# Order of the products in a 576-column matrix multiply, and matmuls that nobody reads in three pauses

## Chip, cores and metric

One core of one Trainium2 chip runs the whole program. The metric is the device time of one launch in microseconds, as a median of several launches: 2850.38 us for the kernel before (three runs, 2848.32 to 2852.73).

## What is computed

One inference step of a two-layer decoder, for a new sequence of 512 tokens and for 8 running sequences of 8 new tokens each. Both sets go through the same weights, so a block of activations has 576 token columns. The reference, cut to what matters:

```python
def _swiglu(h, w_in, w_out):
    gu = h @ w_in
    gate, up = gu[..., :D_FF], gu[..., D_FF:]
    return (jax.nn.silu(gate) * up) @ w_out

for i in range(DEPTH):                                   # DEPTH = 2, D_MODEL = 1024, D_FF = 2816
    x = x + 0.5 * _swiglu(_rms_norm(x, g1), ffn1_w_in[i], ffn1_w_out[i])
    h = _rms_norm(x, mix_norm[i])
    x = x + (gated_delta_net(h) if i < N_A else stick_breaking_attention(h))
    x = x + 0.5 * _swiglu(_rms_norm(x, g2), ffn2_w_in[i], ffn2_w_out[i])
    x = x + (p[i] @ ple_w_in[i]) * sigmoid(_rms_norm(x, gp) @ ple_w_gate[i])
```

After the first layer the shared keys and values are computed; the second layer attends to them and to 256 cached rows of each running sequence.

## The kernel before

**Layout.** Activations lie transposed: 128 of the 1024 features on the partitions, the 576 tokens along the free axis. A weight matrix is taken in blocks of 128 output features (`m` picks one of two output tiles in PSUM) and 128 input features (`k`, up to 8 per tile).

**Exactness.** Inputs are fp32. TensorE's quick type `fp32r` keeps fewer bits, so every operand is split into a high part and a remainder. ScalarE makes the weight's high part (`w_hi`, L462), VectorE the rest (`w_lo`, L477). The activations have the same two halves: `hx_hi` and `hx_lo` after a norm, `hid_hi` and `hid_lo` for a hidden block. A product is then the sum of three: high by high, high by low, low by high.

**The inner loop.** `multiply` (L503) runs over `k`. For each it waits for the activations of that `k` and issues the three products. 576 columns of fp32 don't fit one PSUM bank of 512, so each product is cut in two by `PARTS`: columns 0 to 320, which end one bank, and columns 320 to 576, which begin the next. That is six matmuls for each `k`, all summed into the same tile, and each comes with a weight load of its own. `multiply_pin` (L532) is the same for the embedding product, with 2 steps of `k`. While one tile is multiplied, the other is read out and its weights are split; `evac`, `w_lo_done` and `tile_done` count this.

**Where TensorE pauses.** The engines have queues in program order. In three places the queue of TensorE has nothing to do until others have finished:
- End of the gated DeltaNet stage (`gdn_pe`, L1783 to L1797): sums of squares of the outputs go to ScalarE, come back by token (L1787), go through a square root and a reciprocal, are turned (L1790, L1791), are split, and are spread over the partitions by `norm_spread` (L1474) and `sample_norm_spread` (L1480). VectorE scales the outputs head by head (L1454, L1456) and makes the remainder `hid_lo` (L1460). The first tile of the output projection is multiplied between these: after the product of head `k`, `norm_spread(k + 5)`.
- Start of attention (`attend_pe`, L2376 on): the scores of the first pair of heads and of the new tokens are done, and TensorE waits until ScalarE and GpSimd have turned them into `ls_hi` and `ls_lo` (L1969, L1919) before the suffix sums (`sums`, L2359 to L2362).
- End of attention (L2428 on): the last sequence's cached rows: `att_transposes` (L2297), `page_outputs` (L2310), `o_transposes` (L2319), then the output projection, which waits for `hid_lo` (L2153).

Of the kernel before, what the change touches and what calls it, by code (L numbers as in the profile page):

```python
# [21 lines left out]
P = 128  # L22
# [26 lines left out]
def program(nc, A, O):  # L49
# [33 lines left out]
    with ctx:  # L83
# [419 lines left out]
        def multiply(pe, s, u, m, between=None):  # L503

            k_all = (s.ka, s.kb)[m]
            hi, lo = s.rhs
            n = s.n["unit"]
            pe.wait_ge(w_lo_done, u * 2 + (2 * n + m + 1))
            if isinstance(u, int) and n + u == 0:
                pe.wait_ge(setup_ev, (3, EARLY_FILLS)[m])  # L510
            else:
                pe.wait_ge(evac[m], u + (n, s.n["eb"])[m])
            for k in range(k_all):
                if hi is hx_hi:
                    pe.wait_ge(hx_done, KD * (s.n["hx"] - 1) + k + 1)
                else:
                    pe.wait_ge(hid_done, s.n["hid"] - k_all + k + 1)
                if n + m == 1 and isinstance(u, int) and u == 0 and k == k_all // 2:
                    x_scale_rows(pe)
                if s.stats and n and isinstance(u, int) and u == m == 0 and k == k_all - 1:  # L520
                    pe_stats(pe, s, s.n["stat"])
                for a, (w, h) in enumerate(((w_hi, hi), (w_hi, lo), (w_lo, hi))):
                    for c0, c1 in PARTS:
                        last = nc.tensor.matmul(TILE[m][:, c0:c1], w[:, m, k], h[:, k, c0:c1],  # L524
                                                start=k == 0 and a == 0, stop=k == k_all - 1 and a == 2)
                if between:
                    between(k)
            last.then_inc(tile_done, 1)
            if s.kind == "ple":
                multiply_pin(pe, s, u, m)  # L530

        def multiply_pin(pe, s, u, m):  # L532

            j = KD * s.n["ple"] + m
            pe.wait_ge(pw_lo_done, u * 2 + (j + 1))
            pe.wait_ge(p_done, PK * (s.n["ple"] + 1))
            if not (isinstance(u, int) and 2 * u + j == 0):
                pe.wait_ge(ple_mul, u * 2 + j)
            hi, lo = PR
            for k in range(PK):  # L540
                for a, (w, h) in enumerate(((pw_hi, hi), (pw_hi, lo), (pw_lo, hi))):
                    for c0, c1 in PARTS:
                        last = nc.tensor.matmul(PIN[:, c0:c1], w[:, m, k], h[:, k, c0:c1],  # L543
                                                start=k == 0 and a == 0, stop=k == PK - 1 and a == 2)
            last.then_inc(pin_done, 1)

        def x_scale_rows(pe):

# [58 lines left out]
        def after(eng, *names):  # L607
            for name in names:
                eng.wait_ge(*order[name])
# [874 lines left out]
        def gdn_pe(pe, s):  # L1484
# [106 lines left out]
            def output_sums(heads_, n):  # L1591
                pe.wait_ge(g["osq"], 4 * n + 4)
                for half in range(2):
                    for x, h in enumerate(heads_):
                        last = mm(O_SUMS[32 * x:32 * x + 32, half], hot[:, 15 - h:47 - h], osq[h][:, half * HC:(half + 1) * HC],
                                  start=n == 0, stop=n == 1, skip_group_check=True)
                last.then_inc(g["osum"], 1)
# [31 lines left out]
            for hp in range(NG):  # L1629
# [115 lines left out]
                for i in range(PT):  # L1745
# [33 lines left out]
                    if (hp, i) == (3, 3):  # L1779
                        after(pe, "osum3_s")  # L1780
                        output_sums(FIRST_SUMS, 0)
                        sample_update(3, 7)
            output_sums(LAST_SUMS, 1)  # L1783
            after(pe, "osums")
            for i in range(NT):
                n = P if i < PT else TS
                last = mm(bank(2)[0:n, HA * i:HA * i + HA], o_sums[:, i * P:i * P + n], e32[:, 0:HA], start=True, stop=True)  # L1787
            done("o_by_token", last)
            after(pe, "orec0", "orec1")
            tr(bank(5)[0:32, 0:P], rs_c[:, 0:PT * HA], ident[:])  # L1790
            done("o_scale_rows", tr(bank(5)[0:HA, P:P + TS], rs_c[0:TS, PT * HA:], ident[0:TS, 0:TS]))  # L1791
            after(pe, "ilo0", "ilo1", "upd7_s")
            pe.wait_ge(g["ocp"], HA * PT)
            pe.wait_ge(g["su"], HA * PT)
# [435 lines left out]
        def attend_pe(pe, s):  # L2230
# [143 lines left out]
            far_scores(0)  # L2374
            new_scores()
            pe.wait_ge(at["made"], 5)  # L2376
            for n in range(NP):
                pe.wait_ge(at["lo"], 5 * n + 3)
                sums(n, 0, 2)
                sums(n, 1, 2).then_inc(at["r"], 1)  # L2380
                if n == 1:
                    k_transposes(0, 3)
                for a in range(2):
                    sums(n, a, 3)
                    sums(n, a, 1).then_inc(at["r"], 1)
                if n:
                    page_scores(n - 1)
                    k_transposes(n, 0)
                if n + 1 < NP:
                    near_scores(n + 1)  # L2390
                if n:
                    k_transposes(n, 1)
                for a in range(2):
                    pe.wait_ge(at["lo"], 5 * n + 4 + a)
                    sums(n, a, 0).then_inc(at["r"], 1)
                    if n == NP - 1:
                        k_transposes(n, 2 + a)
                if n == 0:
                    new_sums()
                elif n < NP - 1:  # L2400
                    k_transposes(n, 2)
                pe.wait_ge(hid_done, s.n["hid"] + n)
                pe.wait_ge(at["att"], 5 * n + 3)
                for b in (3, 2, 1):
                    weigh(n, b)
                if n == NP - 1:
                    page_scores(n)
                if n:
                    att_transposes(n - 1)
                if n + 1 < NP:  # L2410
                    far_scores(n + 1)
                if n:
                    page_outputs(n - 1)
                if 0 < n < NP - 1:
                    k_transposes(n, 3)
                pe.wait_ge(at["att"], 5 * n + 5)
                weigh(n, 0).then_inc(at["o_head"], 1)
                if n:
                    o_transposes(n - 1)
                else:  # L2420
                    new_outputs()
                    pe.wait_ge(at["new_out"], 2)
                    k_transposes(n, 0)
                    new_totals(range(0, NB // 2))
                    k_transposes(n, 1)
                    done("totn", new_totals(range(NB // 2, NB)))
                    k_transposes(n, 2)
            att_transposes(NP - 1)  # L2428
            page_outputs(NP - 1)
            o_transposes(NP - 1)  # L2430
            pe.wait_ge(at["o_lo_page"], 2 * NB)
            pe.wait_ge(hid_done, s.n["hid"] + KD)

# [746 lines left out]
```

## Time and profile before

| | |
|---|---|
| median of 3 runs | 2850.38 us |
| the profiled execution | 2854.08 us, span 2852.4 us |
| TensorE matmul, busy | 2768.1 us, 97% of the span, 20784 instructions |
| VectorE, ScalarE, GpSimd, busy | 1343.1, 952.1, 314.9 us |
| mean granted clock of TensorE | 0.984 of full speed |
| DMA | 79 GB/s in the mean, 16 engines about a quarter busy |

A profile of one execution is read here. Its lines name a source line, an engine, what is written and read, and how often. Matmuls are pipelined: a record reaches from the moment one enters the array until its result has drained, so records overlap. The distance between the starts of two is what one costs in a stream. "Granted clock" is the share of TensorE's full 2.4 GHz that the chip allowed at the time; it has two levels here, 1.00 and 0.50 (1.2 GHz). Where a row has brackets, they give the idle time of the engine before it and who ended it.

### The profile page before, as it was taken

The numbers are of one execution on the slowest core, as the hardware profiler recorded it, in microseconds if no ns is written. First come the engines' busy times: TensorE is split into PE (matmuls) and PEld (weight loads), VectorE is DVE, ScalarE is ACT, GpSimd is POOL, SyncE is SP. The second block draws the span as 40 slices with busy tenths as digits, with TensorE's granted clock in tenths as the row PEclk, the third lists the DMA queues.
The fourth block names the chain that finished last, engine by engine and source line by source line (L and its number), as shares of the span: only waits on it lengthen the run. The fifth ranks groups of instructions, "written<-read, shape, count | busy, mean of one in ns | idle before, by whom it ended". The sixth has DMA issues, their size and how long they took to land.

```text
span 2852.4 us, 49966 instructions
## 1 busy us (share of the span) xinstructions
PE 2768.1 (97%) x20784; PEld 2664.3 (93%) x20784; DVE 1343.1 (47%) x1694; ACT 952.1 (33%) x1365; POOL 314.9 (11%) x343
## 2 busy tenths in 40 slices
PE   8999999998999999999999999999989989999998
PEld 8999999997888899999999999999986689999998
DVE  4434347755545554343454434333546744333354
ACT  4212124453333332222342232222336832222243
POOL 2000002201234210000020000000132310000011
PEclk9999999999999899999999999999989999999999
DMA  5222322220011232322231432222212323222231
GB/s 136 74 81 81 89 70 92 77 79 20 18 32 32 91 87 76 88 82 80 74 102 61 135 88 82 81 88 74 89 45 82 131 84 89 83 80 88 74 100 53
DMA packets 308123, 225.71 MB, mean 79 GB/s; under 512 B 8270, under 2 KB 301567, under 8 KB 307967
## 3 DMA queue, kind: packets, MB, share of 16 engines
q1 hardware_dynamic: 307280, 224.26, 26.1%
q8 instruction: 67, 1.10, 0.2%
q14 instruction: 38, 0.31, 0.0%
q0 software_dynamic: 576, 0.00, 0.0%
q10 hardware_dynamic: 162, 0.04, 0.0%
HBM read 212.14 MB, written 12.13 MB: 79 GB/s over the span
## 4 chain that ended last, share of the span: by engine, by line
PE 62%; DVE 2%; ACT 1%; issue 1%; DMA 0%; POOL 0%; SPq 0%; DVEq 0%; POOLq 0%; ACTq 0%
PE ps L524 56%; PE ps L543 1%; PE ps L2325 1%; PE ps L2359 1%; DVE ls L2088 0%; PE ps L2264 0%; PE ps L2367 0%; PE ps L2310 0%; PE ps L1474 0%; PE ps L2361 0%; PE ps L2362 0%; DVE w_lo L477 0%; PE ps L2272 0%; PE ps L2332 0%; PE ps L2288 0%
## 5 line engine op out<-in xcount | busy, mean ns | idle before, releaser
L524 PE MATMUL ps<-hx_hi,w_hi 128*128 128x320 f32 (+1 forms) x3986 | 859.0, 297 | 6.2 <-DVE hx_lo L2453 5.5
L524 PE MATMUL ps<-hx_lo,w_hi 128*128 128x320 f32 (+1 forms) x3986 | 859.1, 296 | 0.0
L524 PE MATMUL ps<-hx_hi,w_lo 128*128 128x320 f32 (+1 forms) x3986 | 845.2, 293 | 0.0
L462 ACT ACTIVATE w_hi<-raw 128x1024 fp32r<-128x1024 f32 (+1 forms) x362 | 375.7, 1038 | 1235.7 <-PE ps L524 1234.9
L524 PEld LDWEIGHTS ps<-hx_lo,w_hi 128*128 128x128 f32 x3986 | 615.2, 190 | 0.0
L524 PEld LDWEIGHTS ps<-hx_hi,w_hi 128*128 128x128 f32 x3986 | 605.4, 188 | 9.9 <-issue 6.4
L524 PEld LDWEIGHTS ps<-hx_hi,w_lo 128*128 128x128 f32 x3986 | 609.7, 188 | 0.0
L477 DVE TENSOR_TENSOR w_lo<-raw,w_hi 128x1024 fp32r<-128x1024 f32 (+1 forms) x362 | 460.8, 1273 | 108.5 <-ACT w_hi L462 108.5
L524 PE MATMUL ps<-hid_hi,w_hi 128*128 128x320 f32 (+1 forms) x1664 | 359.9, 298 | 2.6 <-DVE hid_lo L2153 1.8
L524 PE MATMUL ps<-hid_lo,w_hi 128*128 128x320 f32 (+1 forms) x1664 | 358.6, 297 | 0.0
L524 PE MATMUL ps<-hid_hi,w_lo 128*128 128x320 f32 (+1 forms) x1664 | 357.2, 296 | 0.0
L2470 POOL TENSOR_TENSOR ssum<-ssum,sqb 128x576 f32<-128x576 f32 x64 | 93.3, 1458 | 1966.2 <-issue 1320.2
L524 PEld LDWEIGHTS ps<-hid_hi,w_hi 128*128 128x128 f32 x1664 | 256.1, 190 | 6.1 <-issue 5.4
L524 PEld LDWEIGHTS ps<-hid_lo,w_hi 128*128 128x128 f32 x1664 | 257.6, 190 | 0.0
L524 PEld LDWEIGHTS ps<-hid_hi,w_lo 128*128 128x128 f32 x1664 | 257.5, 190 | 0.0
L2920 DVE TENSOR_TENSOR up_s<-ps,rs 128x576 f32<-128x576 f32 x88 | 66.6, 757 | 344.6 <-PE ps L524 344.6
L2938 DVE SCALAR_TENSOR_TENSOR xT<-ps,xT 128x576 f32<-128x576 f32 x112 | 84.8, 757 | 296.7 <-PE ps L524 296.7
L2917 DVE TENSOR_TENSOR gate_s<-ps,rs 128x576 f32<-128x576 f32 x88 | 66.6, 757 | 258.8 <-PE ps L524 258.5
L2441 ACT ACTIVATE hx_hi<-xT,gain 128x576 fp32r<-128x576 f32 x64 | 48.9, 774 | 163.1 <-DVE xT L2938 163.1
L1014 POOL TENSOR_TENSOR dx<-mt,lm 128x512 f32<-128x512 f32 x56 | 72.6, 1318 | 225.4 <-DVE qkm L1336 156.7
L2784 ACT ACTIVATE hid_hi<-hid_f 128x576 f32 (+1 forms) x88 | 60.5, 687 | 56.1 <-DVE hid_f L2925 56.1
L2453 DVE SCALAR_TENSOR_TENSOR hx_lo<-xT,gain,hx_hi 128x576 fp32r<-128x576 f32 x72 | 58.5, 824 | 43.8 <-ACT hx_hi L2441 43.8
(452 smaller groups left out, 2395.6 us busy)
## 6 DMA issues: line engine op xcount, KB each, us to landing
raw<-in_ffn_w_in SPq DMA_DIRECT2D x176, 512.0 KB, 4.9
raw<-in_ffn_w_out SPq DMA_DIRECT2D x64, 512.0 KB, 4.1
raw<-in_a_w_in SPq DMA_DIRECT2D x33, 512.0 KB, 4.6
raw<-in_ffn_w_out SPq DMA_DIRECT2D x32, 384.0 KB, 3.7
raw<-in_ple_w_gate SPq DMA_DIRECT2D x8, 1024.0 KB, 5.2
raw<-in_w_kv SPq DMA_DIRECT2D x16, 512.0 KB, 4.0
k_page<-in_cache_k SPq DMA_DIRECT2D x16, 512.0 KB, 3.3
v_page<-in_cache_v SPq DMA_DIRECT2D x14, 512.0 KB, 4.7
```

Source lines behind the costliest of these rows:

```text
L462: nc.scalar.activation(w_hi[:, m, 0:k], s.view(m, slot), ACT.Copy).then_inc(w_hi_done, 1)
L477: nc.vector.tensor_tensor(w_lo[:, m, 0:k], s.view(m, slot), w_hi[:, m, 0:k].bitcast(F32), ALU.subtract).then_inc(w_lo_done, 1)
L524: last = nc.tensor.matmul(TILE[m][:, c0:c1], w[:, m, k], h[:, k, c0:c1], start=k == 0 and a == 0, stop=k == k_all - 1 and a == 2)
L543: last = nc.tensor.matmul(PIN[:, c0:c1], w[:, m, k], h[:, k, c0:c1], start=k == 0 and a == 0, stop=k == PK - 1 and a == 2)
L1014: nc.gpsimd.tensor_tensor(L["mo"][:], L["mt"][:], lm[:, level].unsqueeze(1).to_broadcast((P, PT, P)), ALU.mult).then_inc(g["mo"], 1)
L2441: nc.scalar.activation(hx_hi[:, ds(j, 1)], xT[:, ds(j, 1)], ACT.Copy, scale=gain[:, ds(j + s.after, 1)]).then_inc(hx_hi_done, 1)
L2453: nc.vector.scalar_tensor_tensor(hx_lo[:, ds(j, 1)], xT[:, ds(j, 1)], gain[:, ds(j + s.after, 1)], hx_hi[:, ds(j, 1)].bitcast(F32), ALU.mu ...
L2470: nc.gpsimd.tensor_tensor(ssum[:], ssum[:], sqb[:, m], ALU.add).then_inc(ssum_done, 1)
L2784: nc.scalar.activation(hid_hi[:, ds(u, 1)], hid_f[:], ACT.Copy).then_inc(hid_hi_done, 1)
L2917: nc.vector.tensor_tensor(gate_s[:], TILE[0], rs[:], ALU.mult).then_inc(evac[0], 1)
L2920: nc.vector.tensor_tensor(up_s[:], TILE[1], rs[:], ALU.mult).then_inc(evac[1], 1)
L2938: nc.vector.scalar_tensor_tensor(x, TILE[m], s.coef, x, ALU.mult, ALU.add).then_inc(evac[m], 1)
```

## The change

In `multiply` and `multiply_pin` the two inner loops change places: the part of the columns is now the outer loop and the three products the inner one. Each accumulation still begins with its first product and ends with its last; the number of matmuls and weight loads is the same. A new helper, `keep_warm`, issues `n` matmuls of 512 columns whose result nobody reads; it is called 8 times, for 69 matmuls in all: 3, 8 and 4 at the end of DeltaNet (PSUM bank 0), 28 at the start of attention (bank 5), and 12, 4, 2 and 8 at its end (bank 0). Each call stands ahead of a wait.

```diff
@@ multiply
-                for a, (w, h) in enumerate(((w_hi, hi), (w_hi, lo), (w_lo, hi))):
-                    for c0, c1 in PARTS:
+                for c0, c1 in PARTS:
+                    for a, (w, h) in enumerate(((w_hi, hi), (w_hi, lo), (w_lo, hi))):
                         last = nc.tensor.matmul(TILE[m][:, c0:c1], w[:, m, k], h[:, k, c0:c1],
                                                 start=k == 0 and a == 0, stop=k == k_all - 1 and a == 2)
@@ multiply_pin
-                for a, (w, h) in enumerate(((pw_hi, hi), (pw_hi, lo), (pw_lo, hi))):
-                    for c0, c1 in PARTS:
+                for c0, c1 in PARTS:
+                    for a, (w, h) in enumerate(((pw_hi, hi), (pw_hi, lo), (pw_lo, hi))):
                         last = nc.tensor.matmul(PIN[:, c0:c1], w[:, m, k], h[:, k, c0:c1],
@@
+        def keep_warm(pe, n, into):
+            for _ in range(n):
+                nc.tensor.matmul(ps[:, into], ident_r[:], future[:].unsqueeze(1).to_broadcast((P, 4, P)), start=True, stop=True)
@@ gdn_pe
             output_sums(LAST_SUMS, 1)
+            keep_warm(pe, 3, 0)
             after(pe, "osums")
...
             done("o_by_token", last)
+            keep_warm(pe, 8, 0)
             after(pe, "orec0", "orec1")
...
             done("o_scale_rows", tr(bank(5)[0:HA, P:P + TS], rs_c[0:TS, PT * HA:], ident[0:TS, 0:TS]))
+            keep_warm(pe, 4, 0)
             after(pe, "ilo0", "ilo1", "upd7_s")
@@ attend_pe
             pe.wait_ge(at["made"], 5)
+            keep_warm(pe, 28, O_BANK)
             for n in range(NP):
                 pe.wait_ge(at["lo"], 5 * n + 3)
...
+            keep_warm(pe, 12, 0)
             att_transposes(NP - 1)
+            keep_warm(pe, 4, 0)
             page_outputs(NP - 1)
+            keep_warm(pe, 2, 0)
             o_transposes(NP - 1)
+            keep_warm(pe, 8, 0)
             pe.wait_ge(at["o_lo_page"], 2 * NB)
```

## Rows read from the trace of the kernel before

**Rows 1.** The page's groups by cost: executions, busy us, mean ns, idle before
```profile
L524 PE MATMUL ps<-hx_hi,w_hi 128*128 128x320 f32 (+1 forms) x3986 | 859.0, 297 | 6.2 <-DVE hx_lo L2453 5.5
...
L524 PE MATMUL ps<-hid_hi,w_hi 128*128 128x320 f32 (+1 forms) x1664 | 359.9, 298 | 2.6 <-DVE hid_lo L2153 1.8
```

**Rows 2.** TensorE in order of time (start us, us, what), a loop at full clock
```profile
284.60 0.42 PE L524 MATMUL ps<-hid_hi,w_hi 128*128 128x320 f32 x2
...
285.38 0.42 PE L524 MATMUL ps<-hid_hi,w_hi 128*128 128x320 f32 x2
...
286.18 0.43 PE L524 MATMUL ps<-hid_hi,w_hi 128*128 128x320 f32 x2
...
286.98 0.43 PE L524 MATMUL ps<-hid_hi,w_hi 128*128 128x320 f32 x2
```

**Rows 3.** The same view inside attention: neighbours of equal size in one bank
```profile
2276.58 0.28 PE L2359 MATMUL ps<-ls_lo,minus_ones 128*128 128x256 f32 x1
...
2276.70 0.34 PE L2359 MATMUL ps<-ls_hi,minus_ones 128*128 128x384 f32 x1
...
2277.06 0.39 PE L2361 MATMUL ps<-ls_hi,minus_tril 128*128 128x512 f32 x1
...
2277.29 0.40 PE L2362 MATMUL ps<-ls_lo,minus_tril 128*128 128x512 f32 x1
```

**Rows 4.** Stretches: length, busy us of each engine, granted clock, DMA share, GB/s
```profile
956.30:976.70 20.40, 19.38 (x78) 17.69 (x79) 15.05 (x28) 6.68 (x11) 0.00 (x0) 0.50 0.26 83
...
2120.10:2140.70 20.60, 16.18 (x56) 12.66 (x57) 10.86 (x13) 10.06 (x17) 17.15 (x23) 0.50 0.01 0
...
2150.90:2161.20 10.30, 10.30 (x49) 9.94 (x49) 1.74 (x4) 1.18 (x4) 0.00 (x0) 0.50 0.14 52
...
2290.90:2301.10 10.20, 7.64 (x55) 6.70 (x56) 3.78 (x9) 1.22 (x4) 0.58 (x1) 0.50 0.30 103
```

**Rows 5.** TensorE in order of time, end of the DeltaNet stage
```profile
952.98 1.27 PE L1787 MATMUL ps<-e,osq 128*128 128x8 f32 x10 [0.77 <-ACT osq L1150]
956.27 0.37 PE L1790 MATMUL ps<-ident,rs_c 128*32 128x128 f32 x1 [2.02 <-DVE rs_c L1442]
...
957.86 1.08 PE L1474 MATMUL ps<-inv,e_r 64*128 64x128 f32 x4 [1.02 <-DVE inv L1446]
...
973.93 0.68 PE L524 MATMUL ps<-hid_hi,w_hi 128*128 128x320 f32 x2
...
975.38 0.68 PE L524 MATMUL ps<-hid_hi,w_hi 128*128 128x320 f32 x2
```

**Rows 6.** VectorE in order of time, the same place
```profile
973.29 1.59 DVE L1460 TENSOR_TENSOR hid_lo<-osq,hid_hi 128x576 fp32r<-128x576 f32 x2
978.57 0.76 DVE L2938 SCALAR_TENSOR_TENSOR xT<-ps,xT 128x576 f32<-128x576 f32 x1 [3.69 <-PE ps L524]
```

**Rows 7.** VectorE's waits from 957.9 to 974.9: total us, times, longest
```profile
DVE osq L1454 <- PE ps L1474: 1.2, 2, 0.6
DVE osq L1456 <- PE ps L1480: 0.9, 1, 0.9
```

**Rows 8.** TensorE in order of time, start of attention
```profile
2123.74 0.45 PE L2359 MATMUL ps<-ls_hi,minus_ones 128*128 128x128 f32 x1 [7.12 <-POOL ls_lo L1919]
...
2130.41 2.93 PE L2325 MATMUL ps<-qT,kT 64*128 64x384 f32 x10 [0.78 <-ACT att L1973]
```

**Rows 9.** All engines in order of time, end of attention
```profile
2289.61 0.66 PE L2297 MATMUL ps<-ident,att_page_last 128*128 128x128 f32 x4 [3.16 <-ACT att_page_last L1990]
...
2291.14 1.91 PE L2310 MATMUL ps<-v_last,att_keys_last 128*16 128x128 f32 x32 [0.87 <-DVE att_keys_last L2138]
2291.53 2.36 DVE L477 TENSOR_TENSOR w_lo<-raw,w_hi 128x1024 fp32r<-128x1024 f32 x2
...
2293.55 0.69 PE L2319 MATMUL ps<-ident,o_rows 128*128 128x128 f32 x2 [0.49 <-ACT o_rows L1995]
...
2296.05 0.82 PE L524 MATMUL ps<-hid_hi,w_hi 128*128 128x320 f32 x2 [1.82 <-DVE hid_lo L2153]
```

## The prediction

> **What bounds the kernel now.** I read the page's engine shares first: TensorE is 97% busy and no other engine reaches half. A busy TensorE can still be slow, so next came its groups by cost. The main loop's line leads: 3986 + 1664 matmuls of high by high, two for each step of k, so 5650 / 2 = 2825 steps of six matmuls [rows 1]. Then the order of time in a loop: one step begins 0.78 to 0.80 us after the last, 3.17 us for the four that begin with the one before these rows, 0.793 us in the mean, with no bracket of idle time [rows 2]. 2825 x 0.793 = 2240 us of the 2852.4 us span. A nanosecond in each of the six matmuls is 17 us, the largest lever in the kernel. Last I asked for stretches by granted clock. At half clock a step takes 975.38 - 973.93 = 1.45 us [rows 5], and four stretches of 10 to 21 us lie at 0.50, at the end of DeltaNet and around attention [rows 4]. These are the only two things the change can touch.
>
> **The new order of products.** It removes and adds no instruction. In 0.793 us six matmuls stream 3 x (320 + 256) = 1728 columns, which at 2.4 GHz is 0.720 us; 0.073 us is something else, 12 ns a matmul. At half clock the same step is 1.45 us, which is 1728 columns at 1.2 GHz (1.44 us) with next to nothing on top. So the extra time appears only at full clock. What could the order do to it? Three things change: neighbours now go to the same PSUM bank and the same addresses, the stationary block changes four times a step and not twice, and short matmuls stand together.
>
> Attention's sums have all of this already: equal sizes one behind the other, into one bank, added onto the same sums, with weight loads between. A 256-column one holds the engine 2276.70 - 2276.58 = 0.12 us, two of 384 take 0.36 us, one of 512 takes 0.23 us [rows 3]. A line through 256 and 512 gives 0.12 + 64 x 0.11 / 256 = 0.148 us for 320. Three of each are 0.80 us against the measured 0.793 [rows 2]: the alternating order costs what the grouped one costs there, within the rounding of a hundredth. A short matmul (0.12 us) isn't cut off by its weight load either, or the pair of 384 would not keep its 0.18 each. I take zero for the order. The bounds come from the loop itself: steps of 0.78 and of 0.80 us stand side by side [rows 2], with the same instructions on other addresses, so which loads meet which streams is worth about 8 ns either way. In all 2825 steps that is -23 to +25 us (785 and 802 ns at the finest reading of the same four steps).
>
> The Trainium skill, "TensorE: Matmul & The Clock Gate", on back-to-back gaps, gives N / 2.4 GHz plus 2.5 ns for a warm matmul, and says in its step-by-step part that loading the next weights takes nothing from the stream. By that a step would be 735 ns in either order, and an order that reached it would give 164 us back. The trace disagrees with the 735 (793 here), and no row shows an order that comes near it. The same page would make the order worth nothing, which is the value taken above.
>
> **The unread matmuls: what they cost.** Each has 512 columns of fp32r, 0.23 us at full clock [rows 3]. They stand in the queue ahead of a wait, so they cost nothing as long as they fit in it.
> - DeltaNet's end: 3 x 0.23 = 0.69 in a wait of 0.77; 8 make 1.84 in 2.02; 4 make 0.92 in 1.02 [rows 5].
> - Attention's start: 28 make 6.44 in 7.12 [rows 8].
> - Attention's end: 12 make 2.76 in 3.16; 4 make 0.92 in 0.87; 2 make 0.46 in 0.49 (by the idle time of the matmul row); 8 make 1.84 in 1.82 [rows 9].
>
> The sum is 15.9 us in waits of 17.3; the overrun is 0.07 us. The cover is the chain on ScalarE, VectorE and GpSimd, which doesn't need TensorE in these waits. If the clock falls in the middle, the cover is gone: see the rivals.
>
> **The unread matmuls: what they bring.** The four half-clock stretches begin in or just behind pauses. Three are filled. A step costs 0.793 at full clock against 1.45 at half, so busy time at half clock shrinks by 45%. TensorE is busy 19.38, 16.18 and 7.64 us in the three [rows 4], at most 8.8, 7.3 and 3.5 us. Then ask what is late next.
> - DeltaNet's end is paced by VectorE too. In this stretch VectorE waits 1.2 + 0.9 = 2.1 us for TensorE [rows 7] and is otherwise at work on hid_lo. Its last one ends at 973.29 + 1.59 = 974.88, and the tile's result is read at 978.57 [rows 6]. With a warm array the last hid_lo comes 2.1 us earlier, at 972.8, one step and the hand-over (0.9 us) follow, and the tile is read at 973.7: 4.9 us gained.
> - Attention's start is TensorE's own work; the one wait for ScalarE (0.78 us [rows 8]) stays. 7.3 us.
> - Attention's end: the 32 small products take 1.91 us, but VectorE has two w_lo splits queued until 2291.53 + 2.36 = 2293.89, ahead of the sums that follow the transposes. Those end at 2293.55 + 0.69 = 2294.24 [rows 9], so only 0.35 us can be gained there. The projection then runs cold from 2296.05 to 2301.1: 45% of 5.05 is 2.3 us. Together 2.7 us.
> - The fourth stretch, 2150.9 to 2161.2, is not filled. What stands ahead of it is a run of one-column products in `new_totals`, and that stays. Zero, with 45% of 10.30 = 4.6 us as the far bound if it moves.
>
> Sum: 4.9 + 7.3 + 2.7 = 14.9 us. The profiled execution is 2854.08 us, 3.7 above the median of 2850.38. From the profiled time this gives 2839.2, on the scale of the median 2835.5.
>
> **The rivals.**
> 1. *The order helps.* Every step comes down to the quickest that the loop shows, 0.785 us. For it: the 12 ns a matmul above streaming have no cause I can name, and addresses matter [rows 2]. Against it: equal neighbours in attention are no quicker [rows 3]. 2825 x 8 ns = 22.6 us more, 2813.
> 2. *The order hurts: slower than before.* The place is the main loop, the price up to 9 ns a step (802 ns), through twice as many changes of the stationary block or three sums in a row into one bank. 2835.5 + 25 = 2861. It outweighs the warm clock from 14.9 / 2825 = 5.3 ns a step. For it: the spread of steps. Against it: the sums of attention, same bank, cost no more.
> 3. *The change doesn't do what it says: the clock falls anyway.* The unread matmuls multiply the identity by a mostly constant block, and whether that counts as work for the clock no row shows. Then all half-clock time stays, and those that run cold take about 0.42 us (0.23 x 1.45 / 0.793). At attention's start the fall comes at 2120.1, when some 13 are left: 5.5 us from there, 1.9 past the wait's end. At DeltaNet's end 4 of them overrun by 0.7, at attention's end the last 10 by 1.9. 4.5 us slower, 2855, within 0.2% of before.
> 4. *Two of the three hold.* Small products with few rows follow the pauses, and the clock may fall there. 5 to 8 us of the gain is lost: 2842.
>
> **How the numbers follow.** Forecast 0.50, rival 1 0.17, rival 2 0.10, rival 3 0.08, rival 4 0.15. The predicted time is that of the forecast, 2835.5. The range goes down to rival 1 (2812) and up over rival 4 to 2853, which leaves rival 2, most of rival 3 and whatever lies below out, about 0.2. About 0.2%, 5.7 us, is what a measurement of this kernel can tell from no change. Faster by more: forecast, rival 1 and half of rival 4, 0.75. Within: rival 3, the other half of rival 4 less what ends lower, 0.13. Slower: rival 2 and a little of rival 3, 0.12.
>
> **What would show it.** Right: the granted clock of the stretches in [rows 4] is 1.00 but for the fourth, its mean 0.99 or more; a step in a loop is still 0.79 us; the tile behind DeltaNet is read 5 us earlier against its start; the suffix sums' first row has no long wait but unread matmuls ahead of it and begins no later. Wrong: a step that differs from 0.793 by even 5 ns shifts the result by 14 us, as much as all three pauses, and this is the weakest point; a clock of 0.50 right behind the unread matmuls speaks for rival 3.

## The result and the profile after

The changed kernel takes 2831.82 us in the median of four runs (2829.55 to 2834.66), the kernel before 2851.0 on the same chip (2848.32 to 2852.73). The ratio is 0.9924, 95% interval 0.9912 to 0.9936: 19 us faster. The forecast was 2835.5 with a range of 2812 to 2853, so the sign was right and the time lies in the range, 4 us from the forecast. That it lies so near is in part luck: two errors offset each other, and most of the experiments are about these. The profiled execution took 2834.66 us, span 2832.9, mean clock 0.990.

**The three pauses.** Stretches of the kernel after (length, busy us of TensorE matmul, weight load, VectorE, ScalarE, GpSimd, then granted clock, DMA share, GB/s):

```profile
705.20:712.00 6.80, 5.86 (x36) 5.67 (x37) 0.00 (x0) 2.47 (x5) 2.54 (x2) 0.50 0.01 2
783.70:790.50 6.80, 6.80 (x33) 6.36 (x32) 1.38 (x2) 0.98 (x2) 0.00 (x0) 0.50 0.00 0
974.90:978.30 3.40, 3.40 (x14) 3.22 (x14) 1.98 (x4) 0.68 (x1) 0.00 (x0) 0.50 0.35 117
2110.40:2124.00 13.60, 12.29 (x67) 9.56 (x66) 10.46 (x12) 9.33 (x16) 9.45 (x7) 1.00 0.00 0
2138.80:2149.00 10.20, 10.20 (x47) 9.86 (x47) 1.56 (x3) 1.58 (x4) 0.00 (x0) 0.50 0.21 58
2271.00:2290.00 19.00, 17.85 (x136) 15.15 (x135) 9.61 (x19) 6.81 (x15) 0.66 (x2) 1.00 0.25 80
```

Against [rows 4]: attention's start and end are at full clock, the 20.4 us at the end of DeltaNet have shrunk to 3.4, and the fourth stretch stands, with 10.2 us. But two of these rows answer to nothing in [rows 4]: 705 and 784 us lie inside DeltaNet, and there the kernel before was at full clock. DeltaNet has two more differences that are not in these rows: the stretch at its start lasts 10.2 us (from 674.5) and not 6.8 as before (from 679.8), and 3.4 us at half clock from 947.6 are new.

TensorE in order of time in the kernel after (start us, us, what), at the end of DeltaNet, then at the start and at the end of attention. L551 is the unread matmuls:

```profile
955.51 1.18 PE L1601 MATMUL ps<-osq,hot 128*32 128x288 f32 x16
...
956.62 0.96 PE L551 MATMUL ps<-future,ident_r 128*128 128x512 f32 x3
957.46 1.27 PE L1794 MATMUL ps<-e,osq 128*128 128x8 f32 x10
958.66 2.14 PE L551 MATMUL ps<-future,ident_r 128*128 128x512 f32 x8
960.75 0.27 PE L1798 MATMUL ps<-ident,rs_c 128*32 128x128 f32 x1
...
974.66 0.46 PE L524 MATMUL ps<-hid_hi,w_hi 128*128 128x320 f32 x1 [0.45 <-DVE hid_lo L1466]
...
2110.35 6.65 PE L551 MATMUL ps<-future,ident_r 128*128 128x512 f32 x28
2117.53 0.33 PE L2368 MATMUL ps<-ls_hi,minus_ones 128*128 128x128 f32 x1 [0.53 <-POOL ls_lo L1928]
...
2271.68 3.01 PE L551 MATMUL ps<-future,ident_r 128*128 128x512 f32 x12
2275.09 0.66 PE L2306 MATMUL ps<-ident,att_page_last 128*128 128x128 f32 x4 [0.40 <-ACT att_page_last L1999]
...
2280.99 0.39 PE L524 MATMUL ps<-hid_hi,w_hi 128*128 128x320 f32 x1 [0.54 <-DVE hid_lo L2162]
```

The long waits of [rows 5, 8, 9] hold unread matmuls now, and what is left of them is 0.4 to 0.5 us. Behind the pause of attention the scores follow 2121.56 - 2117.53 = 4.03 us after the first suffix sum, against 2130.41 - 2123.74 = 6.67 in [rows 8].

**The steps of the loops.** The same view of the kernel after, once in a loop over `hx` and once over `hid`; each line is the first product of a step, and three are left out between two lines:

```profile
190.15 0.31 PE L524 MATMUL ps<-hx_hi,w_hi 128*128 128x320 f32 x1
...
193.29 0.31 PE L524 MATMUL ps<-hx_hi,w_hi 128*128 128x320 f32 x1
...
284.57 0.31 PE L524 MATMUL ps<-hid_hi,w_hi 128*128 128x320 f32 x1
...
287.76 0.31 PE L524 MATMUL ps<-hid_hi,w_hi 128*128 128x320 f32 x1
```

Four steps take 3.14 us over `hx` and 3.19 over `hid`. In the mean over the full-clock steps, start to start and without the slower first steps of a loop, the kernel before had 793.3 ns in both kinds, the kernel after has 786.7 over `hx` and 796.0 over `hid`. The order was not worth zero: 1993 steps x -6.6 ns = -13.2 us and 832 x +2.6 = +2.2, net -11.0 us.

**Where 19 us went**, by the difference in the start of the same step in both traces (after less before):

| place | difference | since the last |
|---|---|---|
| first steps over `hx` | +1.2 us | |
| before DeltaNet | -3.7 | -4.9 |
| first steps of its output projection | -0.6 | +3.1 |
| before attention | -6.2 | -5.6 |
| first steps behind attention | -17.05 | -10.9 |
| last steps | -19.2 | -2.1 |

DeltaNet gives back 3.1 us although one of the filled pauses is in it. The table compares one execution of each kernel.

### The profile page after: what moved, and what is told of

The parts are those of the page before. It is cut to its first block, busy times and chain, and to the rows that moved or that the text cites. A ratio compares the mean times of both kernels' runs of the same rounds, so it can differ in the third digit from the quotient of the medians.

```text
span 2832.9 us, 50103 instructions
## 1 busy us (share of the span) xinstructions
PE 2760.7 (97%) x20853; PEld 2655.2 (94%) x20853; DVE 1343.1 (47%) x1694; ACT 952.6 (34%) x1365; POOL 314.7 (11%) x343
## 4 chain that ended last, share of the span: by engine, by line
PE 92%; DVE 4%; ACT 1%; issue 1%; POOL 1%; DMA 0%; DVEq 0%; POOLq 0%; ACTq 0%
PE ps L524 78%; PE ps L1731 2%; PE ps L1680 2%; PE ps L543 1%; PE ps L2334 1%; POOL dx L1020 1%; PE ps L2368 0%; DVE ls L2097 0%; PE ps L1593 0%; DVE w_lo L477 0%; PE ps L1739 0%; PE ps L1507 0%; PE ps L2273 0%; DVE xt L1361 0%; PE ps L2376 0%
## 5 line engine op out<-in xcount | busy, mean ns | idle before, releaser
L524 PE MATMUL ps<-hx_hi,w_lo 128*128 128x320 f32 (+1 forms) x3986 | 1172.8, 294 | 0.0
L524 PE MATMUL ps<-hx_lo,w_hi 128*128 128x320 f32 (+1 forms) x3986 | 1172.2, 294 | 0.0
L524 PE MATMUL ps<-hx_hi,w_hi 128*128 128x320 f32 (+1 forms) x3986 | 1164.8, 292 | 7.5 <-DVE hx_lo L2467 5.5
L524 PEld LDWEIGHTS ps<-hx_hi,w_hi 128*128 128x128 f32 x3986 | 749.3, 188 | 10.8 <-issue 6.3
L524 PEld LDWEIGHTS ps<-hx_hi,w_lo 128*128 128x128 f32 x3986 | 749.3, 188 | 0.0
L524 PEld LDWEIGHTS ps<-hx_lo,w_hi 128*128 128x128 f32 x3986 | 748.0, 188 | 0.4
L524 PE MATMUL ps<-hid_hi,w_hi 128*128 128x320 f32 (+1 forms) x1664 | 492.1, 296 | 3.4 <-DVE hid_lo L1466 2.3
L524 PE MATMUL ps<-hid_lo,w_hi 128*128 128x320 f32 (+1 forms) x1664 | 494.6, 297 | 0.0
L524 PE MATMUL ps<-hid_hi,w_lo 128*128 128x320 f32 (+1 forms) x1664 | 490.1, 295 | 0.0
L524 PEld LDWEIGHTS ps<-hid_hi,w_hi 128*128 128x128 f32 x1664 | 314.8, 189 | 7.0 <-issue 4.2
L2952 DVE SCALAR_TENSOR_TENSOR xT<-ps,xT 128x576 f32<-128x576 f32 x112 | 84.9, 758 | 294.0 <-PE ps L524 294.0
```

The source lines that it names most:

```text
L2952: nc.vector.scalar_tensor_tensor(x, TILE[m], s.coef, x, ALU.mult, ALU.add).then_inc(evac[m], 1)
```

## The experiments

Each timing stands beside its own runs of the kernel before, which had a median of 2852.3 to 2852.7 us.

**Each half alone.** The changed kernel without unread matmuls, and the old order with them:

```diff
@@ order_only, against the kernel after
-            for _ in range(n):
+            for _ in range(0):
@@ fills_only, against the kernel after (in multiply, and the same in multiply_pin)
-                for c0, c1 in PARTS:
-                    for a, (w, h) in enumerate(((w_hi, hi), (w_hi, lo), (w_lo, hi))):
+                for a, (w, h) in enumerate(((w_hi, hi), (w_hi, lo), (w_lo, hi))):
+                    for c0, c1 in PARTS:
```

> The changed kernel without its 69 unread matmuls: only the order of the products is new. The two traces side by side say that a step with hx operands fell from 793 to 787 ns and one with hid operands rose from 793 to about 796. Theory (the order is worth that): 1990 x 6.6 = 13.1 us less, 830 x 2.4 = 2.0 us more, so 11 us faster than before, about 2840. The prediction's theory (the order is worth nothing, the pauses bring 15 us): the time of before, 2851. The granted clock falls in the three pauses as before.

> The kernel before with the 69 unread matmuls alone, products in the old order. Theory: what is left of the 19 us once the order has its 11 us, so 8 us faster than before, about 2843; the 15 us of the prediction less what new half-clock stretches inside DeltaNet take back. The prediction's theory: 2836. Steps of the loop take 793 ns as before. Rival (the unread matmuls bring nothing and cost their overrun): 2851 or a little more.

The order alone gave 2849.22 us (twelve runs, 2840.26 to 2850.74), ratio 0.9986 [0.9978, 0.9995]: 3 to 4 us faster where 11 were expected. The unread matmuls alone gave 2843.82 (2839.61 to 2848.43), 0.9968 [0.9955, 0.998]: 9 us. The steps did what they did in the kernel after (786.8 and 796.0 ns in order_only, 793.3 and 793.4 in fills_only), so the order's 11 us are in order_only, and something took 7 of them. TensorE's rows with a wait, inside DeltaNet, in the kernel before and in order_only:

```profile
708.79 2.02 PE L1674 MATMUL ps<-x,dx 128*128 128x128 f32 x16 [2.48 <-ACT x L1124]
```
```profile
705.07 3.75 PE L1680 MATMUL ps<-x,dx 128*128 128x128 f32 x16 [2.48 <-ACT x L1130]
```

The same 16 products behind the same wait of 2.48 us take 2.02 us in one and 3.75 in the other. Stretches of order_only:

```profile
704.30:711.10 6.80, 6.03 (x38) 5.84 (x39) 0.00 (x0) 2.30 (x5) 2.55 (x2) 0.50 0.01 2
782.80:789.60 6.80, 6.80 (x32) 6.35 (x31) 1.38 (x2) 1.14 (x2) 0.00 (x0) 0.50 0.00 0
```

The clock fell about 33 and 112 us into the stage. From its first spread product to its output projection DeltaNet took 288.2 us in the kernel before and 296.1 here: 8 us, about what was missing. In all profiles of the study it is either 285.7 to 288.6 us (no half-clock stretch at these two places) or 293.9 to 296.3 (both, and a third of 3.4 us that begins between 827 and 950). The kernel after is of the second kind (294.0), fills_only too (293.9).

**When DeltaNet begins.** The two kinds share every product of DeltaNet but the 15 unread ones at its end, and its first product begins at times that differ by some us. So in order_only eight unread matmuls were put ahead of the product before the stage, which delays it by 1.8 us of work:

```diff
@@ order_delayed, against order_only, before the "ab" product
+                    if s.kind == "ab":
+                        for _ in range(8):
+                            nc.tensor.matmul(ps[:, 7], ident_r[:], future[:].unsqueeze(1).to_broadcast((P, 4, P)), start=True, stop=True)
```

> [...] Theory (how long DeltaNet and attention take depends on when they begin against the moments at which the clock can change, and launches don't fall evenly on these): the median moves by something else than 1.8 us, most likely down, to 2843 to 2848, with the low runs as frequent as the high ones were. Rival (launches fall evenly): the distribution only moves up by 1.8 us, median 2851.

2838.36 us (2836.88 to 2839.77), 0.9952 [0.9939, 0.9966]: more work, and 11 us faster than order_only. Down was the expected direction, but to 2843 or more. The same places in its trace:

```profile
707.04 2.02 PE L1680 MATMUL ps<-x,dx 128*128 128x128 f32 x16 [2.48 <-ACT x L1130]
```
```profile
710.00:717.00 7.00, 6.76 (x67) 6.29 (x65) 3.29 (x6) 2.36 (x4) 2.16 (x3) 1.00 0.00 0
782.80:789.60 6.80, 6.57 (x55) 6.12 (x55) 1.38 (x2) 2.99 (x5) 2.18 (x2) 1.00 0.01 2
```

DeltaNet took 288.2 us, as in the kernel before. That is 8 us of the 11. Attention took 184.9 us from the scores of its new tokens to the reading of the first tile behind it, against 190.3 in order_only: the stretch at its start was 6.8 us and not 20.5, though the next one was 13.7 and not 10.2. Less 1.8 us for the eight matmuls the two make 11.5. So the same pauses cost more or less, and it is not the work that decides. That it is when they come is borne out by the traces: from the first spread product to the first fall of the clock in DeltaNet it took 2.2 to 2.8 us in all six long profiles, and 1.4 or 3.9 to 4.3 us in all five short ones. The start alone, counted from the start of the program, doesn't sort them (672.04 us in the kernel after, which is long, 672.08 in steps_only, which is short). One run was made to test this, order_delayed. Within one kernel the launches ought then to differ too, and they do, but not evenly: eight of order_only's twelve lie at 2849.2 or above, all five of order_delayed below 2840. Why a kernel falls into one kind nearly every time was not found.

**The order for `hx` alone.**

```diff
@@ order_by_operand, against the kernel after, in multiply alone
-                for c0, c1 in PARTS:
-                    for a, (w, h) in enumerate(((w_hi, hi), (w_hi, lo), (w_lo, hi))):
+                turns = [(c, x) for c in PARTS for x in range(3)] if hi is hx_hi else [(c, x) for x in range(3) for c in PARTS]
+                for (c0, c1), a in turns:
+                    w, h = ((w_hi, hi), (w_hi, lo), (w_lo, hi))[a]
```

> The changed kernel, but the column parts are the outer loop only where the operand is hx; hid and the embedding keep the old order. Theory (the gain and the loss belong to where the operands lie, each on its own): hx steps stay at 787 ns, hid steps go back to 793, 2 us faster than the changed kernel, about 2830. Rival (the order acts on the state of the engine and not on single operands, so one mixed with the other disturbs both): hx steps lose part of the 6.6 ns.

2831.74 us (2826.57 to 2833.36), 0.9931 [0.9918, 0.9944]. The steps came out as expected, 786.8 over `hx` and 793.3 over `hid`; the 2 us that this is worth against the kernel after are not seen in the medians (2831.74 and 2831.82), which differ from run to run by more.

**Addresses.** `hx` and `hid` run the same instructions from other places in SBUF. Three kernels that hold nothing but such steps, on constant data and with no other engine at work, try the places and orders; they compute nothing of the reference.

```python
SHIFTS = [32 * n for n in range(32)]          # probe: where the moving operands lie
OLD = [(c, a) for a in range(3) for c in PARTS]
NEW = [(c, a) for c in PARTS for a in range(3)]
for order in (OLD, NEW):
    for s in SHIFTS:
        for k in range(KD):
            step(s, order, 0, k)
# probe_gaps: the low half moved against the high one by 0 to 224 bytes as well
# probe_orders: 72 orders (which part first, which products in which order) at two places
```

> A kernel of its own that computes nothing of the reference: nothing but steps of six matmuls on constant data, 8 steps (k = 0 to 7) at each of 32 places of the moving operands, 32 bytes apart, first in the old order and then in the new, with the weights where the kernel has them. No other engine works. Theory (a matmul above its streaming time waits for reads of moving operand and next weights that meet in the memory, so it is a matter of addresses): the step's length changes with the place from 780 to 805 ns in both orders; at the place of hx (768 bytes) it is 793 old and 787 new, at that of hid (832 bytes) 793 in the mean with steps from 785 to 802 old, and 796 new. Rival (it is the traffic of the other engines): every step has one length, below 785. Rival (same bank or fewer bank changes): the new order is quicker by the same amount at every place.

> The probe again, computing nothing of the reference: both orders, the high operand at 8 places 32 bytes apart and the low one at 8 distances from it. Theory (addresses): the shortest step isn't the 786.6 ns of the best place so far for all distances; some pair may be shorter, and the longest may pass 805. Rival (786.6 ns is a floor set by the engine): no pair is below 786.

> The probe again, computing nothing of the reference: the operands where hx and hid lie, all 72 orders that keep a column part together (either part first, the three products of each in any order), 8 steps each. Theory (which weight load runs beside which read decides): the orders differ by up to 20 ns a step, and the best order for hx is not the best for hid. Rival (what counts is how often the stationary block changes): orders with the same number of changes take the same time, and those with two changes a step are quickest.

TensorE in order of time in probe: the old order at the place of `hx`, the old order 32 bytes on, the new order at the place of `hx`, and at the place of `hid`:

```profile
190.14 0.42 PE L43 MATMUL ps<-field,w_lo 128*128 128x320 f32 x2
...
193.31 0.42 PE L43 MATMUL ps<-field,w_lo 128*128 128x320 f32 x2
...
196.49 0.42 PE L43 MATMUL ps<-field,w_lo 128*128 128x320 f32 x2
...
199.64 0.42 PE L43 MATMUL ps<-field,w_lo 128*128 128x320 f32 x2
```
```profile
393.18 0.31 PE L43 MATMUL ps<-field,w_lo 128*128 128x320 f32 x1
...
396.33 0.31 PE L43 MATMUL ps<-field,w_lo 128*128 128x320 f32 x1
...
405.82 0.31 PE L43 MATMUL ps<-field,w_lo 128*128 128x320 f32 x1
...
409.01 0.31 PE L43 MATMUL ps<-field,w_lo 128*128 128x320 f32 x1
```

Between the two lines of a pair lie four steps: 3.17, 3.15, 3.15 and 3.19 us. The kernel's difference is there with no other engine working, so no engine, transfer or wait makes it. By place (the pattern repeats every 256 bytes; `hx` is at 0 and `hid` at 64), mean ns of a step (the second to the seventh of eight, so some cells hold steps that had not settled yet):

| place, bytes | 0 | 32 | 64 | 96 | 128 | 160 | 192 | 224 |
|---|---|---|---|---|---|---|---|---|
| old order | 793.3 | 786.7 | 794.7 | 792.5 | 793.5 | 800 | 793.3 | 799.7 |
| new order | 786.6 | 793.3 | 795.1 | 795 | 791.9 | 798.2 | 798.6 | 793.2 |

Neither order is better in itself. Where a step settles, it is mostly at 786.7, 793.3 or 800.0 ns, and in some cases at 780.0, 790.0, 796.7 or 806.7. Elsewhere several steps make one round: at 64 the old order repeats 794, 801, 794 and 785 ns (793.3 in the mean), the new one 790, 796, 800, 796 and 798 (796.0), and these are the means of `hid` in the kernels before and after. So steps of 785 and 801 ns side by side, as in [rows 2], don't come from other places: from one `k` to the next the place modulo 256 stays the same. With the distance of the halves free as well, means lie between 780.0 (new order, place 64) and 806.7 (old order, place 0). Among the 72 orders the change's is among the best for `hx` (786.5; worst 800.8), while for `hid` it gives 796.3 and the best 786.7. How often the stationary block changes doesn't rank them.

**Moving the buffers.** One by the old order and a new place for `hx`, one by the new order and a new place for `hid`:

```diff
@@ shift_only, against the kernel before: no unread matmuls, the old order
         hx0 = whole.at
+        whole.at += 32
         hx_hi = whole.take("hx_hi", [P, KD, T], F32R)
@@ hid_moved, against the kernel after
         hx1 = whole.at
-        whole.at += 32
+        whole.at += 32 + 192
         hid0 = whole.at
```

> The kernel before, old order, no unread matmuls, with hx and all that lies behind it 32 bytes further on. In the probe the old order at 32 takes 786.7 ns, what the new order takes at 0. Theory (the order is worth nothing as such, it only pairs other weight loads with other reads): hx steps fall to 787 ns without any change of order, hid steps (now at 96) to 793, so 13 us of steps less, as in the kernel with the order alone, which measured 4 us less in its time and not 11. If the missing 7 us belong to the order they come back here: 2838. If they belong to where DeltaNet and attention come to lie against the moments at which the clock is set, this kernel can lose them too: 2838 to 2849, with DeltaNet 8 us longer in executions in which the clock falls inside it.

> The changed kernel with hid_hi, hid_lo and all that lies behind them 192 bytes further on in each partition, nothing else. The probe gives the length of a step by the place of its operands, with a period of 256 bytes: hid lies at 64 (832 modulo 256), where the new order takes 795 ns; 192 more is 0, where it takes 786.6. Theory (addresses alone): hid steps fall from 795 to 787 ns, 830 x 8.4 = 7 us faster than the changed kernel, about 2825. Rival (hid steps are longer for another reason, such as the shorter tiles or their other neighbours in time): they stay at 795 and the time at 2832.

shift_only was a miss: 2852.12 us (eleven runs), ratio 0.9998 [0.9988, 1.0008], where 2838, at most 2849, had been expected. Its steps over `hx` take 793.1 ns in the mean and not 787, those over `hid` 792.7. Its trace in two loops over `hx`, with three steps left out between two lines:

```profile
30.88 0.43 PE L525 MATMUL ps<-hx_hi,w_hi 128*128 128x320 f32 x2
...
34.08 0.43 PE L525 MATMUL ps<-hx_hi,w_hi 128*128 128x320 f32 x2
...
189.76 0.42 PE L525 MATMUL ps<-hx_hi,w_hi 128*128 128x320 f32 x2
...
192.91 0.42 PE L525 MATMUL ps<-hx_hi,w_hi 128*128 128x320 f32 x2
```

At the same addresses and in the same order four steps take 3.20 us in one loop and 3.15 in the other, and each loop keeps its length (800, 796.7 or 786.7 ns a step) to its end. So place and order don't fix the length: a loop settles into one of several rhythms, and how it is entered has a part in which. probe_gaps says the same: place 32 in the old order ran at 796.7 there and at 786.7 in probe.

hid_moved held: 2821.43 us (2819.1 to 2824.26), 0.9887 [0.9872, 0.9902]. That is 10 us below the kernel after and the quickest version here but for one that is even with it. A loop over `hid` in it:

```profile
284.06 0.31 PE L524 MATMUL ps<-hid_hi,w_hi 128*128 128x320 f32 x1
...
287.21 0.31 PE L524 MATMUL ps<-hid_hi,w_hi 128*128 128x320 f32 x1
```

3.15 us, not 3.19; the means are 786.7 ns for `hid` and for `hx`. 832 x 9.3 ns = 7.7 us. In the two profiled executions the start of the last step differs by 10.4 us: 7.5 were gained in the loops over `hid` and 7.8 in DeltaNet, where this one had no inner stretches, and some 5 were lost in pieces, 1.1 in DeltaNet's projection and 1.4 in attention among them. So the 10 us are not the moved buffer alone.

**The unread matmuls, with steps and DeltaNet held still.** hid_moved without them (the edit of order_only):

> The kernel with hid moved by 192 bytes and the new order, but without the 69 unread matmuls. Its steps take 787 ns everywhere, 2825 x 6.7 = 19 us less than before. Theory A (steps gained are kept, and the kernel with the order alone lost 7 of its 11 us only through where its DeltaNet and attention came to lie against the moments at which the clock is set): between 2834 and 2842 by the same chance, the traces telling which stages ran at half clock. Theory B (without the unread matmuls quicker steps are given back in the pauses, because the others are then late): the pauses ahead of the half-clock stretches are longer than before, 2841 or more.

2836.77 us (2834.4 to 2840.42), 0.9947 [0.9932, 0.9961], as the steps' own theory had it. Its DeltaNet has no inner stretches either (288.6 us against 286.2 in hid_moved), so this pair gives the cleanest price: 2836.77 - 2821.43 = 15.3 us for the 69 matmuls by the medians. The two profiled executions lie 12.5 us apart, for hid_moved's was the slowest of its four. And against the kernel before, whose profiled DeltaNet is of the same kind, it gives the steps: 15.5 us, where 1993 x 6.6 + 832 x 6.7 ns would be 18.7 and the loops of the two traces differ by 18.2.

**What an unread matmul costs beyond its wait.**

```diff
@@ double_fill, against the kernel after
-            keep_warm(pe, 28, O_BANK)
+            keep_warm(pe, 56, O_BANK)
```

> The changed kernel with 56 in place of 28 unread matmuls at the start of attention. Theory (an unread matmul costs nothing inside its wait and its full 0.23 us beyond): 56 x 0.233 = 13.0 us where the chain of the others takes 7.2, so the first suffix sum comes 5.9 us later against the last score product, 15.0 us behind its start in place of 9.07, and the kernel is 5.9 us slower, the clock staying full. Rival (the array's reads or its writes to the bank slow the others down): more than 6.5 us.

A single execution, 2842.4 us. From the new tokens' scores to the first suffix sum it took 14.74 us against 9.07 in the kernel after: 5.67 more for 28 x 0.229 = 6.41 less the slack left in the wait. Within the wait they cost nothing, beyond it their full length. The kernel was expected 5.9 us slower and is 10.6 above the median of the kernel after. Of the rest, 3.3 us lie in the middle of attention, where this execution has 13.7 us at half clock and the kernel after 10.2. Whether the longer fill has a part in that, one execution doesn't show.

**Two more pauses.** One at the embedding rows of the first layer, one at the norm ahead of the second layer:

```diff
@@ two_more, against hid_moved, where TensorE goes through the stages
+                elif s.kind == "regain":
+                    keep_warm(pe, 20, 4)
                 elif s.kind == "p":
+                    if not s.layer:
+                        pe.wait_ge(const_zero, 8)
+                        keep_warm(pe, 10, 4)
```

> The kernel with hid moved (2821.4 us), with two more pauses filled: 10 unread matmuls ahead of the first transposes of p (a wait of 2.8 us ends at 127 us), 20 ahead of the product for keys and values (a wait of 5.25 us ends at 1504). Theory (a filled pause keeps the clock at full speed and what follows it loses no time): the half-clock stretches at 127 and at 1503 are gone; each held 3 to 6 us of busy TensorE, so 45% of it, 2 to 5 us in all: 2818. Rival (the fill of these pauses delays what follows, or the clock falls anyway): 2821 to 2823.

2820.93 us (2820.42 to 2831.64), 0.9896 [0.988, 0.9912]: even with hid_moved, not 3 us below. The first pause in hid_moved and then in two_more:

```profile
128.35 2.35 PE L3085 MATMUL ps<-ident,p_rows 128*128 128x128 f32 x10 [2.76 <-DVE old_T L2914]
```
```profile
127.25 1.33 PE L3085 MATMUL ps<-ident,p_rows 128*128 128x128 f32 x10 [0.27 <-DVE old_T L2914]
```

The wait is filled and the transposes run at full clock. By the traces the two pauses gained 2.5 to 3.6 and 2.6 us, but the launches don't show it: the three quickest (2820.42 to 2820.93) lie 1 us above hid_moved's two quickest (2819.1, 2819.67), all five at a mean clock of 0.992. The profiled execution was one of the kernel's two long ones (2831.64): in it DeltaNet took 294.1 us, 7.9 more than in hid_moved, and attention 5.6 more, both at half clock.

## Why the prediction was right, and where it was not

- **The order, taken as zero: the failed step.** It was worth -11.0 us, more than half of the result. The line through attention's sums had ends read to a hundredth of a microsecond, 10 ns, and was asked whether six matmuls together differ by 7. Such a line can't answer a question of this size. The bounds (785 and 802 ns) were sound: every mean found in the kernels, 786.7 to 796.0, lies within. So was the sentence named as the weakest point, that 5 ns are worth all three pauses. Rival 1 was half true: `hx` came down by 6.6 ns, nearly its 8. Rival 2 was true for `hid`, with +2.6.
- **The cause.** The prediction spoke of "which loads meet which streams" and gave other addresses for the reason that 0.78 and 0.80 us stand side by side; probe shows such neighbours at one place modulo 256. That the length depends on address and order, with nothing else at work, is shown by probe. Why is open; the meeting of loads and streams wasn't tested by itself. The mean distances to the next start, six in a step over `hx`, are 148, 118, 151, 117, 146, 114 ns before and 146, 145, 148, 113, 118, 118 after, where streaming alone takes 133.3 and 106.7: each matmul has its own surplus, and it moves with the order. At half clock the surplus is gone (1440 ns, 1728 columns at 1.2 GHz), as the prediction read from [rows 5].
- **A step of 735 ns was not reached.** The least of all places, distances and orders tried is 780 ns. The Trainium skill, "TensorE: Matmul & The Clock Gate", section "Back-to-back issue gap", gives N / 2.4 GHz plus 2.5 ns as the gap of an isolated matmul, by which a step is an estimated 735 ns in any order; it adds there that in a stream with weight loads both operations set the spacing. The prediction left that out. The traces disagree with the 735 and with one sum for any order.
- **Attention's start, 7.3 us forecast.** From the first suffix sum to the new tokens' sums it was 16.60 us before and 9.45 after: 7.15. The time ahead, from the new tokens' scores to the first suffix sum, is as long in both (9.08 and 9.07).
- **Attention's end, 2.7 forecast.** From the transposes [rows 9] to the result it was 15.35 us, 2289.61 to the read at 2304.96, and is 12.55: 2.8. VectorE's `w_lo` holds the place as said, for the wait ahead of the projection's first product (6.44 us from the transposes) only shrank to 5.90.
- **DeltaNet's end, 4.9 forecast.** From the second group of output sums to the reading of the tile it was 27.54 us before (951.03 to 978.57) and is 23.51 (955.51 to 979.02), 4.0 less. VectorE in order of time and its waits from 958.6 to 975 us (total, times, longest), kernel after:

```profile
975.36 1.60 DVE L1466 TENSOR_TENSOR hid_lo<-osq,hid_hi 128x576 fp32r<-128x576 f32 x2
979.02 0.76 DVE L2952 SCALAR_TENSOR_TENSOR xT<-ps,xT 128x576 f32<-128x576 f32 x1 [2.06 <-PE ps L524]
```
```profile
DVE osq L1460 <- PE ps L1480: 0.2, 1, 0.2
```

  The 2.1 us for which VectorE waited on TensorE in [rows 7] are down to 0.2, and the last `hid_lo` comes 2.4 us earlier in the stage than in [rows 6] (it ends 21.45 us after the second sums, not 23.85). What is missing is the last hop: the clock fell once more at 974.9, and the last steps ran at half speed. In fills_only, with 13.7 us of half clock there, 2.5 us were gained, in hid_moved, with as much, 2.6. This term was too large in every profile with the fills.
- **The fourth stretch, zero: right.** 10.3 us before [rows 4], 10.2 after.
- **Rival 3: refuted.** At attention's start and end, with the unread matmuls in place, the clock stays at 1.00.
- **Rival 4: true at the end of DeltaNet in four of the six versions with unread matmuls there.** In hid_moved, TensorE in order of time and the stretch:

```profile
953.23 1.20 PE L551 MATMUL ps<-future,ident_r 128*128 128x512 f32 x4
954.38 0.64 PE L1480 MATMUL ps<-inv,e_r 64*128 64x128 f32 x4
...
955.72 2.91 PE L1480 MATMUL ps<-inv,e_r 64*128 64x128 f32 x16
958.55 0.63 PE L524 MATMUL ps<-hid_hi,w_hi 128*128 128x320 f32 x1
```
```profile
956.60:970.20 13.60, 13.60 (x53) 12.46 (x53) 12.49 (x23) 5.94 (x9) 0.00 (x0) 0.50 0.23 78
```

  The unread matmuls ran at full clock, and the clock fell among the small spread products behind them (956.55 us), with no wait of TensorE just before. It fell at the same place in two_more and fills_only too, and in order_by_operand 1.6 us into the projection. In the kernel after and in double_fill it held until 974.9 and 973.7 us. What decides is not shown.
- **What no step had: half clock inside DeltaNet.** Its waits of about 2.5 us are in the trace of before as they are after; there they cost nothing, so no row warned of them. They cost the kernel after about 6 to 8 us, and rival 4, which had the clock fall where small products follow a pause, named this behaviour, but not inside the stage.

The sum by what the profiles show: order -11.0, DeltaNet's end -4.0, attention -7.15 and -2.8, DeltaNet's length +8.3 once its own gain at the end (2.45 up to the first product of the projection) is taken out of 294.0 - 288.2. That is -16.7 of the span's -19.5; a shorter stretch near 127 us, one near 1629 that is gone, and the middle of attention make up the rest, 1 to 1.4 us each, less the 1.2 lost at the start. The forecast's 14.9 came from the fills alone. With the steps and DeltaNet's kind held still these are worth 15.3 by the medians and 12.5 in the two traces, so the term was of the right size, if somewhat large at DeltaNet's end; the order's 11 us, taken as none, then made up for DeltaNet's loss. All of this rests on one profiled execution of each kernel; of which kind their other launches were isn't known.

## What to carry to other kernels

When one loop is four fifths of the time, measure its period to the nanosecond from start times far apart, in each kind of loop, before its order is called free; then try places and orders in a small kernel of that loop, and confirm in the real one, for the length also depends on how a loop is entered. Fill a pause that is followed by TensorE's own small work with matmuls nobody reads, up to the length of the wait and no further. And before a few microseconds are put down to an edit, look at whether the clock fell at the same places in both traces.

## What the runs showed of the hardware

- Six matmuls of 320 and 256 columns, each with its weight load, take 780 to 806.7 ns in the mean, by the operands' place modulo 256 bytes, by their order, and by how the loop was entered. Where single steps settle, most do at 786.7, 793.3 or 800.0 ns; elsewhere four or five steps of 785 to 801 ns make a round (probe, place 64). At 1.2 GHz the period is 1440 ns in the same code.
- At a wait of 2.48 us ahead of 16 products of 128 columns the clock fell in order_only (704.3 us) and not in order_delayed, whose first spread product came 3.0 us later (673.94 against 670.90 us). The price of a pause is thus not a property of the pause: DeltaNet took about 286 to 289 or 294 to 296 us.
- Matmuls of the identity by a mostly constant block hold the clock as other work does (2110.4 to 2124.0 us at 1.00). Behind them it can still fall with TensorE at work without a wait: hid_moved, 956.6 us.
- At half clock TensorE can be busy throughout and stay there: 10.20 of 10.20 us from 2138.8 in the kernel after, 13.60 of 13.60 from 956.6 in hid_moved.
- Open: what makes the periods, why the pattern repeats at 256 bytes, and why a kernel's launches fall mostly into one kind of DeltaNet. The two long runs of five in two_more show that the quickest kernels too are not free of it.
